# Moving a low-half weight split, a residual load and three ScalarE jobs in a one-core streaming encoder step

## The reference

```python
# fox layer
proj = rms_norm(x, g) @ w_in                  # q, k, v, gate (16 heads of 128), forget logit
q, k = rms_norm(q, g_q), rms_norm(k, g_k)
logits = q @ k.T * FOX_SCALE + decay          # masked, causal
o = softmax(logits) @ v * silu(gate)
x = x + o @ w_out
# shared latent, once
c = rms_norm(h @ w_dkv[..., :512]);  kr = rope(rms_norm(h @ w_dkv[..., 512:]))
# MLA layer
kn, v = split(c_all @ w_ukv);  kn = rms_norm(kn, g_knope)      # per head, prompt and cache
logits = (qn @ kn.T + qr @ kr.T) * MLA_SCALE  # masked by chunks of 64
o = softmax(logits) @ v * silu(gate)
y = x + o @ w_out2
```

## Time and profile before

| what | value |
|---|---|
| time, median of three runs | 2170.83 us |
| profiled execution: time, span | 2170.83 us, 2169.0 us |
| PE matmul busy | 2156.2 us (99%) |
| PE weight loads busy | 1867.9 us (86%) |
| DVE busy | 1115.4 us (51%) |
| ACT busy | 952.7 us (44%) |
| POOL busy | 231.6 us (11%) |
| mean DMA busy share in most slices | 20% to 40% |
| granted TensorE clock, mean | 1.000 |

### The profile page before, as it was taken

How to read it: one execution, slowest core, us unless ns; L and a number is a source line. 1 busy time by engine, 2 the same in 40 slices (tenths; PEclk the granted TensorE clock), 3 DMA queues, 4 the chain that set the end, 5 groups by cost and what they waited for, 6 DMA issues and landing times. The chain is left out here.

```text
span 2169.0 us, 33344 instructions
## 1 busy us (share of the span) xinstructions
PE 2156.2 (99%) x11569; PEld 1867.9 (86%) x11569; DVE 1115.4 (51%) x2676; ACT 952.7 (44%) x2242; POOL 231.6 (11%) x255
## 2 busy tenths in 40 slices
PE   8999999999999999999999999999999999999999
PEld 6888888888888888888888988888899999998887
DVE  6645555455555555555233344444377777774222
ACT  5544444444444444453223433344366666664111
POOL 1000000000000000000000001331161010021000
PEclk9999999999999999999999999999999999999999
DMA  5333333333323333333432332433422122122542
GB/s 183 106 103 113 103 103 93 107 107 104 100 90 109 107 103 103 109 106 121 156 112 84 106 107 82 141 124 122 148 78 75 48 63 57 48 65 80 163 131 92
DMA packets 127444, 225.28 MB, mean 104 GB/s; under 512 B 21216, under 2 KB 70624, under 8 KB 127248
## 3 DMA queue, kind: packets, MB, share of 16 engines
q1 hardware_dynamic: 127376, 224.36, 32.5%
HBM read 191.42 MB, written 32.89 MB: 103 GB/s over the span
## 5 line engine op out<-in xcount | busy, mean ns | idle before, releaser
L211 PE MATMUL bank<-b_whi,x_hi 128*128 128x512 f32 x1016 | 401.1, 395 | 0.0
L211 PE MATMUL bank<-b_whi,x_lo 128*128 128x512 f32 x1016 | 396.8, 391 | 0.0
L211 PE MATMUL bank<-b_wlo,x_hi 128*128 128x512 f32 x1016 | 396.7, 390 | 0.0
L194 DVE SCALAR_TENSOR_TENSOR b_wlo<-b_raw,g_fox,b_whi 128x512 fp32r<-128x512 f32 x254 | 179.2, 746 | 143.2 <-ACT b_whi L181 142.7
L181 ACT ACTIVATE b_whi<-b_raw,g_fox 128x512 fp32r<-128x512 f32 x254 | 169.1, 714 | 159.1 <-PE bank L211 134.1
L211 PEld LDWEIGHTS bank<-b_whi,x_lo 128*128 128x128 f32 x1016 | 190.7, 188 | 40.6
L211 PEld LDWEIGHTS bank<-b_whi,x_hi 128*128 128x128 f32 x1016 | 191.0, 188 | 35.8
L211 PEld LDWEIGHTS bank<-b_wlo,x_hi 128*128 128x128 f32 x1016 | 191.0, 188 | 35.5
L211 PE MATMUL bank<-m_whi,x_hi 128*128 128x512 f32 x320 | 125.0, 391 | 0.0
L211 PE MATMUL bank<-m_wlo,x_hi 128*128 128x512 f32 x320 | 124.6, 389 | 0.0
L211 PE MATMUL bank<-m_whi,x_lo 128*128 128x512 f32 x320 | 124.6, 389 | 0.0
(11 more groups left out here) (507 smaller groups left out, 5078.1 us busy)
## 6 DMA issues: line engine op xcount, KB each, us to landing
b_raw<-w_fox SPq DMA_DIRECT2D x127, 512.0 KB, 3.5
m_raw<-w_mla SPq DMA_DIRECT2D x40, 512.0 KB, 3.5
c_raw<-w_out SPq DMA_DIRECT2D x32, 512.0 KB, 3.5
g_raw<-w_out SPq DMA_DIRECT2D x32, 512.0 KB, 3.5
f_raw<-w_ukv SPq DMA_DIRECT2D x16, 512.0 KB, 3.6
queries<-e_q SPq DMA_DIRECT2D x16, 480.0 KB, 4.0
e_raw<-w_uq SPq DMA_DIRECT2D x32, 192.0 KB, 2.4
f_qa<-queries SPq DMA_DIRECT2D x16, 320.0 KB, 3.6
```

Of the source, the lines that this page charges most:

```text
L194: op = eng.scalar_tensor_tensor(lo[:, k, :], raw[:, k, :], self.gain[:, K:K + 1], hi32[:, k, :], ALU.mult, ALU.subtract)
L211: op = eng.matmul(out, a, w[:, k, :], start=(first and k == 0 and i == 0), stop=(last and k == self.kk - 1 and i == len(pairs) - 1))
```

## The change

Three edits, none of which adds or removes work.

1. In stage B the low half of weight unit 2 is made at slot 6 and no longer at slot 3, in the passes that carry a head `g`.
2. On SP `load_res(0)` and the waits in front of it move from inside the loop of `body(None, ...)` (`u == 4`) to behind it.
3. In stage F ACT does `act_values` of banks 0 and 1 at `sb` instead of behind `p3`, `act_new_keys` at `T4` instead of behind those, and `act_keys(3)` at `T7` instead of behind `ont`.

```diff
@@ SP, stage B @@
-                    if h is None and u == 4:
-                        sp.wait_ge(H.out.sem, HEADS * 4 * 16)
-                        H.v_lo.wait(sp, HEADS - 1, 1)
-                        H.gated.wait(sp, HEADS - 1, 1)
-                        H.wait_ready(sp, HEADS - 1, "k")
-                        proj.load_res(sp, 0)
                     if h is None:
                         proj.load_next(sp, 0, u)
...
             body(None, True, HEADS - 1)
+            sp.wait_ge(H.out.sem, HEADS * 4 * 16)
+            H.v_lo.wait(sp, HEADS - 1, 1)
+            H.gated.wait(sp, HEADS - 1, 1)
+            H.wait_ready(sp, HEADS - 1, "k")
+            proj.load_res(sp, 0)
             sp.wait_ge(A.out.sem, 32)
@@ DVE, stage B @@
-                    third = 6 if g is None else 3
-                    if h is not None and (s in (0, third) or (s > 10 and s % 5 == 1)) and not (last and s // 5 == U - 1):
-                        n = 2 if s == third else s // 5 + 1
+                    if h is not None and (s == 0 or (s > 5 and s % 5 == 1)) and not (last and s // 5 == U - 1):
+                        n = s // 5 + 1
                         G.make_lo(dve, h + n // U if n >= U else h, n % U)
@@ ACT, stage F @@
-                        if name in ("T1", "T3", "T5"):
+                        if name in ("T1", "T3", "T5", "T7"):
                             H.act_keys(act_, h, int(name[1]) // 2)
                         elif name == "T8":
                             H.act_new_lo(act_, h)
+                        elif name == "T4":
+                            H.act_new_keys(act_, h)
...
-                        if name == "ont":
-                            H.act_keys(act_, h, 3)
...
-                        if name == "p3":
+                        if name == "sb":
                             if g is not None:
                                 H.wait_out_of(act_, g - 1, "o")
                             H.keys.wait(act_, h, 1)
                             for b in (0, 1):
                                 H.act_values(act_, h, b, par)
-                            H.act_new_keys(act_, h)
```

## The result

The changed kernel takes 2181.98 us, the median of six runs (2181.24 to 2183.44), against 2170.43 us of the kernel before in the same measurement: +11.5 us, ratio 1.0053 with an interval of 1.0040 to 1.0066. It is slower. The forecast was +9.7 us (2180.5 from 2170.83), so the loss is 1.8 us larger than forecast, and the time is inside the range. The profiled execution has a span of 2180.3 us, 11.3 more than before.

What follows compares the result with a forecast made beforehand. PE's matmuls, 99% of the span, were taken as the bound, so moved instructions cost only by making PE wait. 6.8 + 1.1 + 1.9 = 9.8 us on 2170.83 gave 2180.6, stated as 2180.5; range 2176 to 2186.

Steps and rivals of the forecast that it cites:

- Edit 1, loop passes: Stage B, first load of unit 2: 2.21 us of delay against 1.85 slack, 0.41 us later in 14 passes, 5.7 us.
- The lateness of unit 4's load: SP loads unit 4 2.2 us later; costed at nothing, if uncovered up to 2.2 us more a pass.
- Edit 1, the pass with head 0: Stage B, load of unit 2 in the tighter pass: 84.9 against 83.79, +1.1 us.
- 81.2 + 2.21: Pass with head 0: earliest start after the norm, plus the five moved-up DVE instructions' time, taken from a loop pass.
- Edit 2: At the barrier: `c_res` lands after the last `c_raw` load, DVE adds late, PE starts at 1021.3 instead of 1020.19, +1.1 us.
- Edit 3: Stage F, ACT's new order: 0.15 us per head for 14 heads, about 0.2 less in the last, +1.9 us.
- 0.07 + 0.27 - 0.19: Stage F, per head: 0.07 left from `p1` after absorption at `g`, 0.27 before `o`, 0.19 regained before `kp`.
- the hidden stall: Rival, stage B: slack larger than it looks, slot 9's load starts at 321.15 all the same; 2173.8 us, chance 0.08.
- the gain through `g`: Rival, stage F: earlier squares make the scaled gate ready, the 0.33 us before `g` goes in 14 heads; 2166 us, chance 0.03.
- the one without absorption: Rival, stage F: MLA waits do not absorb each other, +0.5 us a head, +7 instead of 1.9; 2185.5 us, chance 0.05.
- The clock: Rival: PE's clock falls behind each of 15 new waits, 3 us each, +45; about 2226 us, chance 0.02.

Runs made afterwards that it cites:

- e8_gate_early_after: The changed kernel, with DVE's scaling of the gate moved to behind the low half of `p3`: 2179.24 us, ratio 1.0037 to the kernel before.

## Why the prediction was right, step by step

The direction, the mechanisms and their places held. Three sizes did not: edit 1 was forecast 0.7 us too small (6.8 against 7.46) and edit 3 1.4 too small (1.9 against 3.28), edit 2 was forecast 0.4 too large, and 0.45 us came where nothing was forecast. That the sum is only 1.8 us off owes a little to edit 2's error, which has the other sign.

- *Edit 1, loop passes:* 0.41 a pass forecast, 0.42 at the load in question (0.27 in the last pass, which the forecast priced like the others), and 0.43 to 0.45 from pass to pass. 5.7 forecast, 5.83 alone and 6.04 within the change. The lateness of unit 4's load cost nothing, as assumed: there is no other step in a pass.
- *Edit 1, the pass with head 0:* 1.1 forecast, 1.42 measured. The step that was short is "81.2 + 2.21". This execution runs 0.47 us ahead at that time, so the values should have started at 80.73; they started at 80.96, and took 2.34 us to the low half instead of 2.21:

```profile
80.96 0.88 DVE L831 TENSOR_TENSOR b_v<-b_raw,b_v 128x512 fp32r<-128x512 f32 x2
81.76 0.67 DVE L833 TENSOR_TENSOR b_cvs<-b_cv,b_cvs 128x512 fp32r<-128x512 f32 x1
82.36 1.00 DVE L841 SCALAR_TENSOR_TENSOR b_gate<-b_gate,b_raw 128x512 f32<-128x512 f32 x2
83.30 1.40 DVE L194 SCALAR_TENSOR_TENSOR b_wlo<-b_raw,g_fox,b_whi 128x512 fp32r<-128x512 f32 x2
```

  The 0.23 and the 0.13 are the missing 0.3. The prediction took the 2.21 us from a loop pass, where POOL does nothing beside these instructions; here it does: see the last section.
- *Edit 2:* 1.1 forecast, 0.66 within the change and 1.33 alone. The chain was right (issue behind 9.49 us, landing, three additions, 0.47 to PE); the landing took 7.1 and 7.7 us where the forecast took 7.5. One landing of each is on record, so which of the two is usual stays open.
- *Edit 3:* per loop head 0.07 + 0.27 - 0.19 = 0.15 forecast. Measured in the head that ends at 1722: +0.28 before `p1` and -0.18 at `g`, so 0.10; +0.30 before `o`; -0.17 before `kp`; 0.23 in sum. All three are off by 0.02 to 0.03 in the same direction, and times 14 that is most of the 1.4 us by which stage F came out above 1.9 (3.28). Part of it need not be the edit's: edit 3 alone makes a loop head 0.20 longer, and traces without an edit in this stage differ by up to 0.03 a head.
- *The rest:* 0.4 us appears in the changed kernel alone at 1567, at the first load of stage E, with no releaser in the trace. No single edit shows it, and neither does `e8_gate_early_after`, which has all three. So it is not the price of the edits together but of one execution, from a cause that stays open, as do the 0.46 us that edit 2 alone shows in stage F.

Of the rivals, the hidden stall is out by the wait of 0.38 that DVE releases, the gain through `g` by the wait of 0.21 that is left there, and the one without absorption by the head of 0.23 instead of 0.5; the run that took the cover away came to 0.35. The clock stayed at 1.00 behind all 15 waits of edit 1, each of them right behind ten transposes: the pass above shows 1.00 over its whole length, and from the second matmul behind the wait on the starts are 0.23 to 0.24 us apart. The rule of the Trainium skill that was weighed for this rival (TensorE: Matmul & The Clock Gate, "Part 4: PE-mode transpose") cost nothing here.

## What to carry to other kernels

Read the slack of a moved instruction at the load that waits for it, in each copy of the loop, not in the loop alone: 1.41 us of delay were free, 2.21 us cost 0.42 each time, and the pass with head 0 had less to give. Where the bounding engine never rests, the excess is paid in full and simply adds up; where it has a wait a little later, that wait takes part of the new one, and this can be shown by removing the old wait. A move on one engine's list is worth nothing while the consumer stands behind another wait on its own list: with ACT's list alone the wait before `kp` grew, with DVE's moved too it was gone. The first pass of a loop can have another order and needs its own look: there the same move cost 2.06 us at once. And the residual load was free ahead of the last blocking weight load in its queue, also 19 us late, and not behind it.

## What the runs showed of the hardware

DVE and POOL can make each other's instructions longer. In the pass with head 0 the norm's instruction takes 0.34 us, and 0.55 from the time when POOL adds the mask to the decay; POOL's start hangs on a DMA, and it came at 79.53 before and at 78.75 in the changed kernel. So the last instruction of the norm stands behind four slowed ones there, and behind two before: from the norm's first start to its last 3.21 us instead of 2.79. The changed kernel:

```profile
78.54 0.34 DVE L824 SCALAR_TENSOR_TENSOR b_raw<-b_raw,b_rstd,gq 128x128 f32<-128x128 f32 x1
78.81 0.56 DVE L824 SCALAR_TENSOR_TENSOR b_raw<-b_raw,b_rstd,gk 128x128 f32<-128x128 f32 x1
79.28 0.55 DVE L824 SCALAR_TENSOR_TENSOR b_raw<-b_raw,b_rstd,gq 128x128 f32<-128x128 f32 x1
```
```profile
78.75 1.87 POOL L1046 TENSOR_TENSOR b_decay<-b_decay,mask_fox 128x128 f32<-128x128 f32 x4 [1.30 <-DMA b_decay_new<-decay]
```

The starts are 0.47 us apart there instead of 0.26. POOL's additions start 0.42 to 0.47 us apart beside them, and 0.42 apart where DVE is idle. Every one of the five traces that were read at this place has three or more such instructions beginning within 0.3 us of POOL's start, and none before it.

It can also be POOL that pays. Its addition to the 64 sample rows takes 0.31 to 0.34 us in all 16 passes before, each time with DVE idle beside it, and 2.03 us once in the changed kernel, in this pass, where DVE's last norm, the values and the first gate instruction run in one row beside it:

```profile
81.57 0.32 POOL L1049 TENSOR_TENSOR b_decay_new<-b_decay_new,mask_fox 64x64 f32<-64x64 f32 x1
```
```profile
80.59 2.03 POOL L1048 TENSOR_TENSOR b_decay_new<-b_decay_new,mask_fox 64x64 f32<-64x64 f32 x1
```

Of these DVE instructions only the last, during which POOL's ended, is longer than elsewhere (0.80 us instead of 0.68): that is the 0.13 of above.

That the two engines want the same way into memory is argued from this; no run was made for it. The Trainium skill (SBUF — State Buffer, "Who interferes with whom") says that an instruction of VectorE with two inputs in SBUF contends with one of GpSimd that reads SBUF. The norm has two, and the 0.55 against 0.34 agrees.
